# Eight modulation slabs multiplied and summed by GpSimd instead of TensorE, in a two-layer transformer block kernel

## The reference

```python
mod_x = (jax.nn.silu(c) @ w_ada[l] + b_ada[l])[:, None, :]
mod_c = (jax.nn.silu(c_ctx) @ w_ada[l] + b_ada[l])[None, None, :]
sh_a, sc_a, g_a, sh_m, sc_m, g_m = jnp.split(mod_x, N_MOD, axis=-1)
hx = _modulate(_rmsnorm(x, norm_attn[l]), sh_a, sc_a)
...
x = x + g_a * _merge(ya, yb, ga, gb, w_oa[l], w_ob[l], w_out[l])
hx = _modulate(_rmsnorm(x, norm_mlp[l]), sh_m, sc_m)
x = x + g_m * moe(hx.reshape(b * s, d)).reshape(b, s, d)
```

## Time and profile before

| what | value |
|---|---|
| median of 3 runs | 1860.28 us (1856.88 to 1860.4) |
| the profiled execution | 1859.85 us, span 1858.0 us |
| TensorE busy | 1775.7 us (96%) |
| VectorE busy | 749.4 us (40%) |
| ScalarE busy | 576.6 us (31%) |
| GpSimd busy | 20.3 us (1%) |
| DMA, mean | 303 GB/s |

### The profile page before, as it was taken

The page is one execution under the profiler, slowest core; times in us unless marked ns, Lnnn a source line. Parts: engine busy times, 40 slices in busy tenths (PEclk is TensorE's granted clock), DMA queues, the critical chain, the costliest instruction groups (busy, mean ns, idle before and its releaser), DMA issues.

```text
span 1858.0 us, 23003 instructions
## 1 busy us (share of the span) xinstructions
PE 1775.7 (96%) x9486; PEld 1042.7 (56%) x9486; DVE 749.4 (40%) x1359; ACT 576.6 (31%) x1044; POOL 20.3 (1%) x59
## 2 busy tenths in 40 slices
PE   5999999999999999999999999989999999999999
PEld 4987787333333333333232323338788887788887
DVE  2654655111211111111111111135677776667776
ACT  4445574111011011001010110135654446565443
POOL 1020010000000000000000000000000000000000
PEclk9999999999999999999999999999999999999999
DMA  8664557999999999999999999995335636334551
GB/s 311 233 233 154 200 198 316 363 427 427 427 428 426 428 428 426 427 428 427 426 428 427 427 428 426 428 363 195 123 137 199 209 137 247 107 122 160 203 181 46
DMA packets 122043, 563.09 MB, mean 303 GB/s; under 512 B 7216, under 2 KB 53424, under 8 KB 97360
## 3 DMA queue, kind: packets, MB, share of 16 engines
q1 hardware_dynamic: 121104, 558.70, 75.1%
q10 hardware_dynamic: 832, 2.89, 0.4%
HBM read 560.52 MB, written 1.05 MB: 302 GB/s over the span
## 4 chain that ended last, share of the span: by engine, by line
PE 76%; DMA 18%; DVE 3%; ACT 2%; issue 1%; SPq 0%; ACTq 0%; DVEq 0%
PE ps L1105 15%; PE ps L1128 10%; DMA arena<-in_w_up 9%; PE ps L1383 9%; PE ps L665 8%; PE ps L666 8%; PE ps L667 8%; DMA ring<-in_w_up 7%; PE ps L1384 4%; PE ps L1063 2%; PE ps L1043 2%; DMA ring<-in_w_ada 1%; PE ps L677 1%; PE ps L984 1%; DMA ring<-in_w_in 1%
## 5 line engine op out<-in xcount | busy, mean ns | idle before, releaser
L2077 DVE TENSOR_TENSOR part<-ring,part 128x1024 fp32r<-128x1024 f32 (+2 forms) x299 | 320.6, 1091 | 163.3 <-ACT part L1510 162.9
L665 PE MATMUL ps<-part,part 128*128 128x512 f32 (+1 forms) x888 | 314.8, 355 | 5.6 <-DVE part L2077 3.6
L666 PE MATMUL ps<-part,part 128*128 128x512 f32 (+1 forms) x888 | 303.8, 342 | 0.0
L667 PE MATMUL ps<-part,part 128*128 128x512 f32 (+1 forms) x888 | 303.6, 342 | 0.0
L1510 ACT ACTIVATE part<-ring 128x1024 fp32r<-128x1024 f32 (+2 forms) x299 | 272.4, 945 | 94.9 <-DVE ring L2077 69.6
L1105 PE MATMUL ps<-ring,arena 128*64 128x512 f32 x1216 | 269.9, 595 | 9.0 <-DMA ring<-in_w_up 8.7
L1383 PE MATMUL ps<-part,part 128*128 128x512 f32 x704 | 250.2, 399 | 0.0
L2074 DVE TENSOR_SCALAR arena<-ps 128x512 f32<-128x512 f32 x64 | 44.3, 692 | 427.9 <-PE ps L1105 427.9
L1384 PE MATMUL ps<-part,part 128*128 128x256 f32 x704 | 197.5, 281 | 0.0
L665 PEld LDWEIGHTS ps<-part,part 128*128 128x128 f32 x888 | 169.8, 191 | 39.3 <-issue 12.3
L1105 PEld LDWEIGHTS ps<-ring,arena 128*64 128x64 f32 x1216 | 84.3, 137 | 191.4 <-issue 169.1
(11 more groups left out here) (268 smaller groups left out, 1432.9 us busy)
## 6 DMA issues: line engine op xcount, KB each, us to landing
ring<-in_w_down SPq DMA_DIRECT2D x39, 2048.0 KB, 35.4
ring<-in_w_up SPq DMA_DIRECT2D x38, 2048.0 KB, 35.9
ring<-in_w_gate SPq DMA_DIRECT2D x38, 2048.0 KB, 35.0
arena<-in_w_up SPq DMA_DIRECT2D x26, 2048.0 KB, 36.7
ring<-in_ffn_w_in SPq DMA_DIRECT2D x44, 1024.0 KB, 7.9
arena<-in_w_down SPq DMA_DIRECT2D x18, 2048.0 KB, 36.3
spare<-in_w_gate SPq DMA_DIRECT2D x13, 2048.0 KB, 35.2
arena<-in_w_gate SPq DMA_DIRECT2D x13, 2048.0 KB, 34.5
```

The costliest lines, as they stand in the source:

```text
L665: e.matmul(out, x[0], y[0], start=first, stop=False, skip_group_check=True)
L666: e.matmul(out, x[0], y[1], start=False, stop=False, skip_group_check=True)
L667: return e.matmul(out, x[1], y[0], start=False, stop=last, skip_group_check=True)
L2077: return e.tensor_tensor(out, x, y, op)
```

## The change

- **Slabs 4 to 11** are multiplied by GpSimd. For each of a slab's 8 lines it multiplies the line in place by the line's column of silu(c) (`tensor_scalar`, 128x512), and adds lines 1 to 7 to line 0 (`tensor_tensor`, 128x512). These are 64 and 56 instructions, and they stand ahead of the angles in GpSimd's program. `ada_features` then sums over the 128 partitions on TensorE, 4 products with a column of ones, at the steps in `ada_column` (9, 12, 17, 20, 23, 26, 29, 32). The 64 products of `ada`, ScalarE's 8 row copies and the 32 products of `ada_columns` for these slabs go, too; only x's modulation comes out (both columns alike).
- **Slots.** Slabs 4 to 11 use slots 1 and 6 in turn, and their slot is free only when the columns are summed. The first expert load (`("first", 0)`, slot 6) moves from behind slab 7 to behind slab 11. The slots of the projections, of the experts and of the second part are renamed to fit.
- **Gate evictions** wait for the scores of units 3, 7, 13 and 15, at the first, third, fifth and seventh.
- `scores(0)` waits for slab 4's modulation instead of slab 6's, the first `turn_p` for slab 5's also, since their columns stand in those PSUM banks.
- **Stage e**, VectorE's step 17: the first half's rotation, head 1's diagonals and head 2's maximum stand ahead of the split of piece 20.

```diff
--- before.py
+++ after.py
-                slot = (0, 3, 2, 1)[next(turn) % 4]
+                slot = (2, 3, 1, 0)[next(turn) % 4]
...
-        slabs = {"kva": (512, 256, 2), "qa": (0, 512, 3), "kb": (1280, 512, 2), "qb": (768, 512, 0), "vb": (1792, 512, 1),
-                 "ga0": (2304, 512, 2), "ga1": (2816, 512, 0), "gb0": (3328, 512, 1), "gb1": (3840, 512, 0)}
+        slabs = {"kva": (512, 256, 2), "qa": (0, 512, 3), "kb": (1280, 512, 2), "qb": (768, 512, 0), "vb": (1792, 512, 2),
+                 "ga0": (2304, 512, 0), "ga1": (2816, 512, 2), "gb0": (3328, 512, 0), "gb1": (3840, 512, 2)}
         for key in (("ada", 0, 0), ("ada", 2, 1), ("in", "kva"), ("ada", 1, 0), ("ada", 3, 1), ("in", "qa"), ("in", "kb"), ("ada", 4, 1),
-                    ("in", "qb"), ("ada", 5, 1), ("in", "ga0"), ("in", "vb"), ("ada", 6, 0), ("in", "ga1"), ("ada", 7, 1), ("first", 0, 6),
-                    ("ada", 8, 1), ("ada", 9, 2), ("in", "gb0"), ("in", "gb1"), ("ada", 10, 2), ("ada", 11, 2), ("o", "oa", 1),
-                    ("out", 0, 2), ("o", "ob", 0), ("first", 1, 4), ("out", 1, 1)):
+                    ("in", "qb"), ("ada", 5, 6), ("in", "vb"), ("ada", 6, 1), ("in", "ga0"), ("ada", 7, 6), ("in", "ga1"), ("ada", 8, 1),
+                    ("in", "gb0"), ("ada", 9, 6), ("in", "gb1"), ("ada", 10, 1), ("o", "oa", 0), ("ada", 11, 6), ("o", "ob", 2),
+                    ("out", 0, 1), ("first", 0, 6), ("first", 1, 4), ("out", 1, 0)):
...
-        ada_step = {4: 5, 5: 8, 6: 11, 7: 16, 8: 19, 9: 21, 10: 24, 11: 27}
-
-        def ada_bank(s):
-            return {0: 4, 1: 6, 2: 5, 3: 7}[s] if s < 4 else 6 if s < 7 else 2
-
-        def ada_rows(s):
-            return a.rows[s] if s < 4 else a.rows[s % 2] if s < 7 else a.t2
+        ada_column = {4: 9, 5: 12, 6: 17, 7: 20, 8: 23, 9: 26, 10: 29, 11: 32}
+
+        def ada_columns_at(s):
+
+            return PS[{4: 6, 5: 7}.get(s, 2)][:, 8 * (s - 4):8 * (s - 4) + 8]
...
-        order = itertools.cycle((6, 4, 0, 3, 5, 2, 1, 7, 8, 9))
+        order = itertools.cycle((6, 4, 2, 3, 5, 1, 0, 7, 8, 9))
...
-                return [s_ada.of(key[1])]
+                return [s_ada.of(key[1]) if key[1] < 4 else s_col.of(key[1])]
...
+            def ada_features(s):
+                e.wait_ge(*s_scaled.of(s, 7))
+                if s != 5:
+                    e.wait_ge(*({4: s_mod.of(1), 6: s_vev.of("vb0", 0)}[s] if s in (4, 6) else s_mod.of(s - 1)))
+                for j in range(4):
+                    i = e.matmul(ada_columns_at(s)[:, 2 * j:2 * j + 2], W(("ada", s))[:, 0, 128 * j:128 * j + 128], C("one", 2),
+                                 start=True, stop=True, skip_group_check=True)
+                i.then_inc(*s_col.up(s))
...
-                    e.wait_ge(*s_mod.of(6))
+                    e.wait_ge(*s_mod.of(4))
...
+                    e.wait_ge(*s_mod.of(5))
...
-                for s, step in ada_step.items():
-                    if step == t - 1:
-                        ada_columns(s, ada_bank(s), ada_rows(s))
+                for s, step in ada_column.items():
+                    if step == t:
+                        ada_features(s)
...
                 if v is not None and v < 8:
                     turn_p(v, 1)
-                for s, step in ada_step.items():
-                    if step == t:
-                        e.wait_ge(*({4: s_mod.of(1), 7: s_vev.of("vb0", 0)}[s] if s in (4, 7) else s_mod.of(s - 1)))
-                        ada(s, ada_bank(s))
...
-                    if i in (0, 4):
-                        e.wait_ge(*s_qk.of(7 if i == 0 else 15))
+                    if i % 2 == 0:
+                        e.wait_ge(*s_qk.of((3, 7, 13, 15)[i // 2]))
...
-                for s, step in ada_step.items():
-                    if step == t:
-                        if s > 4:
-                            e.wait_ge(*s_col.of(s - 1))
-                        ada_row(s, ada_bank(s), ada_rows(s))
...
+                    if t == score_at(h) + 1 and h != 2:
+                        head_max(h)
                 if t == 17:
+                    m_rotate(3, 0)
+                    head_diagonals(1)
+                    head_max(2)
                     low(E0 + 20)
...
-                    for q in range(2):
+                    for q in (1,) if i == 3 else (0, 1):
                         m_rotate(i, q)
...
+                    if t == score_at(h) + 1 and h != 1:
+                        head_diagonals(h)
...
+            e.wait_ge(*s_silu.of())
+            for s in range(4, 12):
+                w = W(("ada", s))
+                e.wait_ge(*loaded(("ada", s)))
+                for k in range(8):
+                    e.tensor_scalar(w[:, k, :], w[:, k, :], a.c32[:, k, 0:1], None, ALU.mult).then_inc(*s_line.up(s, k))
+                    if k:
+                        e.wait_ge(*s_line.of(s, k))
+                        if k > 1:
+                            e.wait_ge(*s_scaled.of(s, k - 1))
+                        e.tensor_tensor(w[:, 0, :], w[:, 0, :], w[:, k, :], ALU.add).then_inc(*s_scaled.up(s, k))
+
```

More of the change, by code:

```diff
@@ L75, in shape_constants @@
     put("inv", np.tile(half, (128, 1)))
-    for name, value in (("eps", EPS), ("eps64", 64 * EPS), ("eps128", 128 * EPS), ("eps5", 1e-5), ("one", 1.0)):
+    for name, value in (("eps", EPS), ("eps64", 64 * EPS), ("eps128", 128 * EPS), ("eps5", 1e-5)):
         put(name, np.full((128, 1), value, np.float32))
+    put("one", np.ones((128, 2), np.float32))
     put("sel2", (i[:, None] % 32 == np.arange(2)[None, :]).astype(np.float32))
@@ L2270, in vector_program @@
                     low_a(t + 4)
-                for s, step in ada_step.items():
+                for s, step in ada_column.items():
                     if step == t - 1:
-                        mod_add(s, ada_bank(s))
+                        mod_add(s, ada_columns_at(s))
                 for i in now:
```

59 lines of the change are left out of this document (30 added, 29 removed).

## The result

The changed kernel takes **1879.51 us** (median; 1879.24 to 1881.62, 4 runs) where the kernel before takes 1860.34: a ratio of 1.0109, 95% interval 1.0093 to 1.0126. It is slower by 19 us, 1.1%; the forecast was 1848, and 1867 was the end of its range. The profiled execution took 1881.62 us, its span is 1879.8.

A forecast was written before the change was run, and what follows sets the result against it. TensorE was taken to bound stage a, a microsecond off it there being worth one at the end. 1859.85 - 25.9 (gains) + 5 (late slabs) + 8.8 (VectorE's waits) = 1847.75, so 1848 us; range 1835 to 1867.

The forecast's parts named there:

- The gains: TensorE in stages a and e: eight slab products, slab 6's wait, two gate-eviction waits and stage e's wait go, 25.9 us.
- GpSimd's time per slab: Stage a: 8 multiplications and 7 additions take 16.4 us alone (bounds 12.4 and 20.4), 22.5 us beside VectorE.
- The contention on GpSimd: Stage a: GpSimd stands still during VectorE's two-SBUF-input operations, lengthening a slab from 16.4 to 22.5 us, at most 25.6.
- When the slabs are due: Stage a: TensorE waits for GpSimd's slabs near steps 12 and 32, 5 us in all with the slower clock.
- the second rival: GpSimd's slab chain bounds stage a; L is its time per slab, deciding from 24 us; 1868 us at L = 25, chance 0.17.
- What the slow clock costs: Stage a: 1 us more for the slower clock behind TensorE's wait for slab 11.
- VectorE's waits: Steps 21 to 28: VectorE waits for GpSimd's operations, 1.1 us a step, 8.8 us; steps 14 to 20 taken as free.
- Moved at no cost: SyncE's loads, first expert load and angles move later at 0 us; the angles up to 5 if slabs are late.
- The exclusion costs nothing: Rival: VectorE wins against GpSimd, slabs take 18 us, all 25.9 us come, 1834 us; chance 0.22.
- The second part doesn't gain: Rival: in stage e another wait replaces head 2's, 1852 us; inside the forecast's own range, no separate chance.
- GpSimd becomes the bound of stage a: Rival: the slabs' single chain on GpSimd makes stage a late, kernel slower, 1868 us at 25 us a slab; chance 0.17.
- waits for GpSimd over 10 us in sum: Sign that the forecast is wrong; it expected few TensorE waits for GpSimd, 2 to 4 us, near steps 12 and 32.

The follow-up runs named there:

- e4: Changed kernel, but TensorE neither waits for nor reads GpSimd's slab sums, and GpSimd scales only one element a slab: 1832.55 us, ratio 0.9875.
- e1: Kernel before with only the gate evictions changed, to wait for the scores of units 3, 7, 13 and 15: 1856.4 us, ratio 0.9991.
- e2: Kernel before with the changed gate evictions and VectorE's new order in step 17 of the last attention, no slab on GpSimd: 1852.86 us, ratio 0.997.
- e10: Changed kernel with GpSimd scaling and summing six of each slab's eight lines: 4090.99 us, unreadable as the router took the long path; only stage a's trace is used.
- e11: Changed kernel with TensorE kept busy by unused products in its waits for slabs 5, 10 and 11: 1878.9 us, ratio 1.01.
- e3: Changed kernel with GpSimd's slab work kept, but TensorE neither waits for it nor reads it: 1872.58 us, ratio 1.0068.
- e5: Changed kernel with GpSimd's 64 products made by a two-input operation, c repeated along the line: 1877.1 us, ratio 1.0095.
- e8: Kernel before with GpSimd running single operations of 128, 512 and 1024 elements on a free slot from about 60 us, to price them: 1862.09 us, one execution.
- e14: Changed kernel with only slabs 7 to 11 on GpSimd, 4 to 6 back on TensorE, and GpSimd's products by a two-input operation: 1864.61 us, ratio 1.0029.
- e6: Changed kernel, TensorE neither waiting for nor reading GpSimd's slab sums, with the angles moved from behind slab 11 to behind slab 6: 1867.91 us, ratio 1.005.
- e13: Changed kernel with only slabs 7 to 9 on GpSimd, slabs 4 to 6, 10 and 11 given back to TensorE: 1846.83 us, ratio 0.9931.

## Why the prediction was wrong

*The gains.* **Right** in sum: 25.9 us forecast, 25.4 measured (e4, 20 to 27). By parts: in the changed kernel's stage e the wait of the earlier trace rows is 0.5 us, and the second part is 2.7 to 4.9 us shorter, for 4.1 forecast. The two waits behind the gate evictions are gone. Their 5.9 us are there at equal clock (e1); over all runs the medians differ by 1.5 us, within the noise, and no step of mine had the clock in it. The slab products, 15.9 with the wait for slab 6, gave 14.7 at the router's rows (294.0 in e2, 279.3 in e4); by the medians it is 20.3 from e2 to e4, of which 3.3 are a slow stretch that e2's profile has at the border and e4's doesn't. e4's executions have the mean clock of the kernel before beside them (0.9954 both), e2's a lower one (0.9943): the sum shows whole in e4 and not in e2.

*GpSimd's time per slab.* **This is the step that failed**: 22.5 us taken, 25.7 measured, by the sum "8 x 0.8 + 7 x 1.26 + 15 x 0.08 = 16.4". The sum of two lines was right (1.26, measured 1.27). The product wasn't: "a multiplication lies between 0.29 and 1.30; I take 0.8, since it reads one operand less". It takes 1.56, outside my bounds. My upper bound took the slope of the operation with two inputs, 2.1 ns an element, for one with a scalar, whose slope is (1.56 - 0.29) / 480 = 2.6. A slab alone is thus 8 x 1.56 + 7 x 1.27 + 7 x 0.08 = 21.9 us. The kernel before has no row that shows it; a product of more than 32 elements on GpSimd wasn't in it.

*The contention on GpSimd.* Too high: 6.1 us a slab taken, 25.7 - 21.9 = 3.8 measured. It hid part of the first error. With my 0.8 and the measured 3.8 a slab would be 19.6 us; e10's take 19.2 (150.3 us busy by eight, and its gaps), and cost TensorE one wait of 2.4 us. An estimate from e4 and e10, 1832.6 + 13.0 = 1846 us, says what the change would then have taken: my 1848.

*When the slabs are due.* The working was right, and steep as the second rival said. From L = 24 each microsecond costs eight. Its 1868 for L = 25 had the chain end at 259.5; it ended at 269.05, 9.6 later (5.4 by L = 25.7, 3.3 by the idling for slab 8, which that sum had left out, 0.9 by the start). Less the 3 us that it gave to the angles, for which nothing waited, and with the slow clock behind slab 11 and at the border (2.7 and 3 us), which it had not: 1868 + 9.6 - 3 + 5.7 = 1880, measured 1879.5 to 1881.6. Against e4 the changed kernel is 42.5 us late at slab 11's columns (269.1 and 226.6) and 45.2 at the router's rows. I had seen the wait and given it 0.17.

*What the slow clock costs.* I had 1 us for it. Behind the last wait it is 2.7 (e11), and 3 at the border in this profile; what lies ahead of slab 11 counts only as far as it makes GpSimd idle, since the chain sets the time: 1.5 us of idling, and 2.9 at the chain's end (e11).

*VectorE's waits, 8.8 us.* **About right in size**, and hidden in the result: e3 shows 6.7 us in steps 21 to 28, and 11.5 with what comes ahead of them (3.7, in steps 6 and 15) and behind, which I had at nothing. In the changed kernel it lies inside the waits for GpSimd. The Trainium skill ("SBUF — State Buffer", Who interferes with whom) has VectorE with two SBUF inputs and a GpSimd operation that reads SBUF exclude each other for the whole instruction. Where both have two inputs the trace agrees (1.58 and 1.10 us for 1.22 and 0.25; all nine low parts that came up in the middle of a sum were held). Where GpSimd's is the product with a scalar it does not: thirteen of the fifteen low parts that came up in one were not held, and the product at 92.87 stood still for the low part. In e5, with products of two inputs, all ten were held (1.46 us or more, 1.95 on average). It is no clean rule either: two low parts were held by a product (1.51 and 1.63 us), in e8 three that came up in the first 0.35 us of a product with a constant took 1.35 to 1.87, and the scaling of p was held by products too. So the product that is slow alone is the better neighbour, and exchanging it gained nothing in e5 and cost 15 to 18 us in e14.

*Moved at no cost.* For the time before and after of this change, right: nothing waited for the angles or for the queue. But they were free only because TensorE stood waiting for slab 11 anyway. With that wait gone the angles cost 21 us (e3) and the order of loads 19.7 (e6). My "up to 5 if the slabs are late" was a quarter of that.

*The rivals.* "The exclusion costs nothing" fell (10 to 11.5 us). "The second part doesn't gain" fell (2.7 to 4.9 us gained). "GpSimd becomes the bound of stage a" is what happened, and "waits for GpSimd over 10 us in sum" was the sign that I had named for it.

**Open**: why the clock falls more often in some kernels, at the border between stages above all, without a long idle stretch ahead like those behind which it falls in stage a; whether three or five slabs are better; and, within 4 to 6 us, what five gain over none.

## What to carry to other kernels

Work that is taken from the busiest engine and strung on an idle one is a chain: write down when each link is due and the link's length from which the chain decides, and where that length rests on a price that no row shows (here 8 of 15 operations), the chance belongs to the price's bounds and not to its middle. Then follow everything that waits for the end of the chain, on every queue, since removing one customer only shows the next. An engine whose work and another's hold each other up is to be priced by whom it holds up: put its work where the neighbour has room, and prefer the operation that yields, even if it is slower; here five slabs of eight, with room, gain 4 to 6 us where eight lose 26 (1847 and 1879.5 beside 1853).

## What the runs showed of the hardware

- GpSimd's product with a scalar takes 1.56 us on 512 elements (1.49 with a constant, 2.77 to 2.85 on 1024), more than a product of two inputs (1.04, the second repeated along the line) or a sum of two lines (1.27 to 1.31); a copy takes 0.61.
- VectorE's low part (two SBUF inputs, 1.22 us alone) took 1.58 to 2.32 us where it came up in the middle of a GpSimd sum, 1.95 on average in a product of two inputs, and 1.21 to 1.23 in thirteen of fifteen cases in a product with a scalar. VectorE's scaling by a column (0.49 us alone) took 0.89 in six of eight cases in a product with a scalar.
- Even VectorE's work with two SBUF inputs on one element a partition gets longer: the mean of 32 went from 155 to 288 ns, and to 474 with all of GpSimd's operations of two inputs.
- Executions of one program differ by up to 13 us (1850.2 to 1863.7 in e1) nearly in order of their mean granted clock, 0.997 to 0.990; a stretch of 10 us at 1.2 GHz just ahead of or at the start of the experts is there in some kernels' profiles (changed, e2, e13) and not in others' (before, e4).
